# Two transformer models in one kernel: tiles moved by 32 bytes, query norms moved into the softmax exponent, steps cut in two

## What is computed

```python
def rmsnorm(x, g):
    y = xf * lax.rsqrt(jnp.mean(xf * xf, axis=-1, keepdims=True) + EPS)
    return y * g

def memory_cross(qm, k_mem, v_mem, q_gain, k_gain):     # layers 0 and 1, and alike in the second model
    q = rmsnorm(qm.reshape(b, s, N_MEM_HEADS, HEAD_DIM), q_gain) * HEAD_DIM ** -0.5
    k = rmsnorm(k_mem, k_gain)
    logits = jnp.einsum('bshd,bmhd->bhsm', q, k)
    p = jax.nn.softmax(logits, axis=-1)
    return jnp.einsum('bhsm,bmhd->bshd', p, v_mem)

# window attention of the second model: q and k normed, rotated, a sink in the softmax
    m = jnp.maximum(jnp.max(s, axis=-1, keepdims=True), sink)
    p = jnp.exp(s - m)
    denom = jnp.sum(p, axis=-1, keepdims=True) + jnp.exp(sink - m)
```

## Time and profile before

| | |
|---|---|
| median of 3 runs | 2280.51 us (2278.16 to 2287.36) |
| the profiled execution | 2279.7 us |
| its span | 2277.9 us |
| TensorE matmul busy | 2153.2 us (95%) |
| weight loads busy | 1778.0 us (78%) |
| VectorE busy | 1268.2 us (56%) |
| ScalarE busy | 934.3 us (41%) |
| POOL busy | 33.7 us (1%) |
| mean granted TensorE clock | 0.973 |
| DMA queue's share of the span | 25.4% |

### The profile page before, as it was taken

The page is one execution under the profiler, slowest core; times in us unless marked ns, Lnnn a source line. Parts: engine busy times, 40 slices in busy tenths (PEclk is TensorE's granted clock), DMA queues, the critical chain, the costliest instruction groups (busy, mean ns, idle before and its releaser), DMA issues.

```text
span 2277.9 us, 30665 instructions
## 1 busy us (share of the span) xinstructions
PE 2153.2 (95%) x11378; PEld 1778.0 (78%) x11378; DVE 1268.2 (56%) x2177; ACT 934.3 (41%) x1908; POOL 33.7 (1%) x71
## 2 busy tenths in 40 slices
PE   6899899999998777999999999999998779999999
PEld 6888688878888666888888888888887558888887
DVE  7545557736754664577377545344548735543542
ACT  6655444424435664444244333223343444332331
POOL 0000001000000000000000000000001000000000
PEclk9999899999999798999999999999999889999999
DMA  6211022332222000223322233323222003332332
GB/s 203 67 60 48 29 88 89 102 99 96 93 94 92 15 16 6 91 94 101 98 91 99 98 97 95 98 94 97 93 88 61 15 15 97 94 99 95 94 100 88
DMA packets 101669, 187.35 MB, mean 82 GB/s; under 512 B 11408, under 2 KB 12048, under 8 KB 101264
## 3 DMA queue, kind: packets, MB, share of 16 engines
q1 hardware_dynamic: 101520, 185.39, 25.4%
HBM read 183.25 MB, written 2.10 MB: 81 GB/s over the span
## 4 chain that ended last, share of the span: by engine, by line
PE 79%; DVE 8%; ACT 5%; issue 2%; DVEq 0%; ACTq 0%
PE PS L1391 22%; PE PS L1393 22%; PE PS L1392 22%; PE PS L1409 2%; PE PS L1410 2%; PE PS L1411 2%; PE PS L1511 2%; PE PS L1479 2%; PE PS L1497 2%; DVE WL L1553 1%; ACT PP L1865 1%; PE PS L1520 1%; DVE PSTAT L1650 1%; DVE RS L1542 1%; ACT WH L1796 1%
## 5 line engine op out<-in xcount | busy, mean ns | idle before, releaser
L1553 DVE TENSOR_TENSOR WL<-RAW,WH 128x512 fp32r<-128x512 f32 x681 | 458.6, 690 | 313.3 <-ACT WH L1796 291.7
L1391 PE MATMUL PS<-HNh,WH 128*128 128x512 f32 x1440 | 562.6, 391 | 0.7 <-DVE WL L1553 0.7
L1393 PE MATMUL PS<-HNh,WL 128*128 128x512 f32 x1440 | 560.3, 389 | 0.0
L1392 PE MATMUL PS<-HNl,WH 128*128 128x512 f32 x1440 | 560.2, 389 | 0.0
L1796 ACT ACTIVATE WH<-RAW 128x512 fp32r<-128x512 f32 x681 | 414.4, 626 | 331.7 <-PE PS L1393 223.0
L1391 PEld LDWEIGHTS PS<-HNh,WH 128*128 128x128 f32 x1440 | 270.3, 188 | 58.4 <-issue 2.4
L1392 PEld LDWEIGHTS PS<-HNl,WH 128*128 128x128 f32 x1440 | 270.3, 188 | 57.3 <-issue 1.2
L1393 PEld LDWEIGHTS PS<-HNh,WL 128*128 128x128 f32 x1440 | 270.3, 188 | 56.3
L1391 PE MATMUL PS<-Gh,WH 128*128 128x512 f32 x704 | 278.2, 395 | 0.8 <-DVE Gl L1707 0.8
L1393 PE MATMUL PS<-Gh,WL 128*128 128x512 f32 x704 | 278.1, 395 | 0.0
L1392 PE MATMUL PS<-Gl,WH 128*128 128x512 f32 x704 | 278.1, 395 | 0.0
(11 more groups left out here) (244 smaller groups left out, 2448.4 us busy)
## 6 DMA issues: line engine op xcount, KB each, us to landing
RAW<-in_w SPq DMA_DIRECT2D x681, 256.0 KB, 2.6
XT<-in_x SPq DMA_DIRECT2D x8, 256.0 KB, 5.3
MT<-in_mem SPq DMA_DIRECT2D x2, 1024.0 KB, 6.6
out_x<-XT SPq DMA_DIRECT2D x8, 256.0 KB, 2.0
PAR<-in_par SPq DMA_DIRECT2D x1, 207.0 KB, 7.9
CB<-in_cb SPq DMA_DIRECT2D x1, 100.0 KB, 7.8
PAR<-in_par SPq DMA_DIRECT2D x1, 84.5 KB, 2.0
CONST<-in_const SPq DMA_DIRECT2D x1, 65.0 KB, 6.0
```

What stands on the lines that cost most here:

```text
L1391: pe.matmul(out, wh, xh, start=(a["start"] and c == 0), stop=False)
L1392: pe.matmul(out, wh, xl, start=False, stop=False)
L1393: p = pe.matmul(out, wl, xh, start=False, stop=ends)
L1553: dve.tensor_tensor(l[:, :], r[:, :], h[:, :], ALU.subtract).then_inc(done.sem("split.dve"), 1)
```

## The change

1. **Places.** `FILL` gives 80 floats to a new tile `QR` [128, 5, 16] of roots; `FILL2` has 60 floats in place of 68. In the built program every tile from `KMH` to `PAR` then starts 32 bytes lower, at a multiple of 2048 (`KMH` 110592, `AOH` and `Gh` 137216, `AOL` 153600, `Gl` 159744). The tiles before `KMH` stay.
2. **Roots in the exponent.** Memory queries (all three) and window queries are turned as they come from `evac` (or from POOL's rotation), through a new function `unscaled`; their 10 `tnorm` are gone. The roots go to `QR`. `pmax` multiplies the negated maximum by the root, [128, 1] by [128, 1] (48 new instructions for memory pairs; for the 32 with sinks the `min` becomes one instruction that multiplies and takes the minimum), and `pexp` gets the root as a second pointer operand, the scale (80 exponents).
3. **Steps in two.** `rnorm` becomes `rlog` and `rnorm`, `qsplit` becomes `qhigh` and `qsplit`, `pmix` becomes `pmul` and `pmix`, with 0.9 to 1.5 units between, so VectorE has other steps in between.
4. **Smaller moves.** `recip` stands ahead of the copies of the fourth tile, not 0.1 units after. The latents' turns start 2.2, 4 and 5.5 units after the copy, not 0.2, 1.4 and 2.6.

```diff
-        sb("FILL", [128, 512 - 136 - 128 - 16 - 32])
+        QR = sb("QR", [128, 5, 16])
+        sb("FILL", [128, 512 - 136 - 128 - 16 - 32 - 80])
...
-        sb("FILL2", [128, 68])
+        sb("FILL2", [128, 60])
...
                 def rest():
+                    need(job.roots[1] if job.roots else [])
...
                 def copies():
+                    if i == 3:
+                        self.recip(n)
                     for x in range(2):
                         step(("pcopya", "pcopyb")[x], key + (x,), job=job, i=i, bank=banks[x], PT=PT[x], free=free)
-                    if i == 3:
-                        after(0.1, lambda: self.recip(n))
...
+                step("pmul", key, last=(self.id, n, 3), F=F, h=h, free=free)
+                after(1.2, lambda: step("pmix", key, F=F, h=h, l=l))
...
+        def roots(g, F, h, S, out=None, lag=1.5):
+            c = F.roots[h][0]
+            out = S[:, 3, c] if out is None else out[:, c]
+            step("rlog", (g, h), S=S, c=c, parts=F.roots[h][1],
+                 got=[("ssum.dve", (g, x)) for x in (range(len(F.squares)) if len(F.roots) == 1 else (h,))])
+            after(lag, lambda: step("rnorm", (g, h), S=S, c=c, out=out))
+
+        def unscaled(g, F, got, dsts, h, keep, lag=1.0):
+            if h == 0:
+                ss.take(g, [("rnorm.dve", (g, len(F.roots) - 1))])
+            squares(g, F, h, got(h))
+            ready_at = got(h)
+            if F.rots:
+                y, A, B, M = F.rots[h]
+                step("trope", (g, h), y=y, A=A, B=B, M=M, got=[("ssq.act", (g, h))])
+                ready_at = ("trope.pool", (g, h))
+            if h == len(F.squares) - 1:
+                for x in range(len(dsts)):
+                    after(lag + 1.5 * x, lambda x=x: turn(g, x, ready_at, dsts[x]))
+
+            def total():
+                sums(g, F, h, SS[ss.of[g]][:, 0, F.squares[h][3]], ss.before[g])
+                after(1.2, lambda: roots(g, F, h, SS[ss.of[g]], keep))
+            after(1.5, total)
...
-                step("qsplit", (g, x), src=PS[aux][0:rows, 0:n], h=h, l=l, gain=gain, free=tokens)
+                step("qhigh", (g, x), src=src, h=h, gain=gain, free=tokens)
+                after(0.9, lambda: step("qsplit", (g, x), src=src, h=h, l=l, gain=gain))
...
-                after(0.2 + 1.2 * x, lambda x=x, gain=gain: turn(g, x, ("evac.act", (g, 0)), (
+                after((2.2, 4, 5.5)[x], lambda x=x, gain=gain: turn(g, x, ("evac.act", (g, 0)), (
...
+                            m = stt(top, top, root(i, x), NSINK[:, h:h + 1], ALU.mult, ALU.min)
+                        else:
+                            m = dve.tensor_tensor(top, top, root(i, x), ALU.mult)
...
+                                   scale=a["job"].roots[0](i, x) if a["job"].roots else 1.0, accum_out=St[:, x, 1, i:i + 1]).then_inc(done.sem("pexp.act"), 1)
```

More of the change, by code:

```diff
@@ L739, in mix @@
                 need(free)
-                step("pmix", key, last=(self.id, n, 3), F=TMP[tmp.of["pmix", key]], h=AOH[:, job.chunk, :],
-                     l=AOL[:, job.chunk, :], free=free)
+                F, h, l = TMP[tmp.of["pmix", key]], AOH[:, job.chunk, :], AOL[:, job.chunk, :]
+                step("pmul", key, last=(self.id, n, 3), F=F, h=h, free=free)
+                after(1.2, lambda: step("pmix", key, F=F, h=h, l=l))
             def run(self):
@@ L955, in root @@
                 for h in list(range(len(F.roots)))[part]:
-                    step("rnorm", (g, h), S=S, c=F.roots[h][0], parts=F.roots[h][1],
-                         got=[("ssum.dve", (g, x)) for x in (range(len(F.squares)) if len(F.roots) == 1 else (h,))])
+                    roots(g, F, h, S)
                 after(lags[2], scale)
@@ L1031, in gates @@
             after(6, cum)
-        mq_got = [("qsplit.dve", (dense_at[0], c)) for c in range(2)]
+        g_mq0, mq_got = dense_at[0], [("qsplit.dve", (dense_at[0], c)) for c in range(2)]
         after(15.9, lambda: norm.columns(0))
@@ L1037, in mq_use @@
             gates(g)
-            heads(g, by_heads(Y, 4), lambda h: ("evac.act", (g, 0)), mq_chunks(0, par("mq0"))(Y))
+            for h in range(2):
+                unscaled(g, by_heads(Y, 4), lambda h: ("evac.act", (g, 0)), mq_chunks(0, par("mq0"))(Y), h, QR[:, 0, :])
         wide(norm, "fox", MQ_COLS, [PS[t][:, 0:268] for t in range(4)], range(4),
@@ L1202, in root @@
                 def root():
-                    step("rnorm", (g, 0), S=S, c=F.roots[0][0], parts=F.roots[0][1],
-                         got=[("ssum.dve", (g, x)) for x in range(len(F.squares))])
+                    roots(g, F, 0, S)
                     after(3, scale)
@@ L1317, in q_use @@
         def q_use(p):
-            return lambda g, Y, h: heads(
+            return lambda g, Y, h: unscaled(
                 g, by_heads(Y, 4, Q_ROT), lambda h: ("evac.act", (g, h)),
                 [(chunks_of(Y, 4, x), BQ[0][:, 2 * p + x, :], BQ[1][:, 2 * p + x, :], par("gq2"), lambda: [])
-                 for x in range(2)], h, h + 1)
+                 for x in range(2)], h, QR[:, 3 + p, :], 2.0)
         tiles = [(0, 128, [(0, MCAUS)])] + [(128 * (i - 1), 256, [(0, MPREV), (128, MCAUS)]) for i in range(1, 4)]
@@ L1325, in program @@
         jobs = [Pair([(BQ[0][r, n, :], BQ[1][r, n, :]) for r in (lo, hi)], [(BK[0][r, :], BK[1][r, :]) for r in (lo, hi)],
-                     VB[:, :, :], tiles, n, pair_got[n], sink=(n, 4 + n), wants=3) for n in range(4)] + mem_pairs(1, 4, mq_got)
+                     VB[:, :, :], tiles, n, pair_got[n], sink=(n, 4 + n), wants=3) for n in range(4)]
+        roots_of = {what: dense_at[0] + n for n, what in enumerate(BLK_GROUPS)}
+        for n, j in enumerate(jobs):
+            g = roots_of["q", 512 + 256 * (n // 2)]
+            j.scaled_by(QR[:, 3 + n // 2, :], lambda i, x, n=n: 4 * i + 2 * (n % 2) + x, [("rnorm.dve", (g, h)) for h in range(2)])
+        jobs += mem_pairs(1, 4, mq_got, QR[:, 2, :], roots_of["mq", 1280])
         for j in jobs[4:]:
@@ L1596, in vector @@
                     x.then_inc(done.sem("rnorm.in"), 1)
+                elif k == "rnorm":
+                    z, R = (a["S"][:, i, a["c"]] for i in (1, 2))
                     w.wait_ge(*done("rnorm.act", key))
```

65 lines of the change are left out of this document (38 added, 27 removed).

## The result

| | before | after |
|---|---|---|
| median of the runs, us | 2280.06 (4 runs) | 2246.02 (4 runs, 2243.52 to 2246.95) |
| ratio | | 0.9843, 95% interval 0.9820 to 0.9866 |
| profiled execution, us (its span) | 2279.7 (2277.9) | 2246.5 (2244.7) |
| last Gl matmul to first AOL matmul, latent layer | 693.0 to 902.8: 209.8 | 690.7 to 887.8: 197.1 |
| the same, second model | 1677.87 to 1858.12: 180.2 | 1655.24 to 1828.57: 173.3 |

The change gained 34 us, 1.5%; 2248 was forecast. Of the 33.2 us of the spans, 12.7 + 6.9 - 1.9 = 17.7 came from the attentions and 15.5 from everything else. The total is right.

The account below looks back on a forecast made before the run. TensorE's matmul-to-matmul time bounds the streaming stretches; waits between engines and a lowered clock bound the attentions. -18.4 - 2.4 - 7 - 5 = -32.8 from 2279.7 gives 2246.9, the median 0.8 higher: 2248 us, range 2234 to 2267.

Parts of the forecast that it names:

- Part 1: Tiles from KMH on start at multiples of 2048 bytes: Gl and AOL save 20.5 ns per weight tile, -18.4 us.
- part 4, cut steps: All attentions: cutting steps in two frees VectorE while ScalarE rounds; no gain counted where VectorE isn't the bound.
- part 4, reciprocal: All attentions: reciprocal ahead of the last turned tile's copies, TensorE's broadcast waits 0.45 us less each, -5 us.
- earlier memory tiles: Layer with latents: first memory score can come 8 us sooner, half of it counted, -4.2 us.
- hole: Second model's attention: memory tiles follow the last values at once, filling TensorE's 14.4 us before the memory scores, -8 us.
- VectorE's stretch: Second model's attention, where VectorE is the bound at first: six scalings go and waits in the root are filled, -4 us.
- rotation: Second model's attention: window queries' turns wait for POOL's rotation alone, +1 us where it is slow.
- products and pointers: Product of maximum and root plus the exponent's second pointer operand: +3.3 us in the latent layer, +4 in the second model.
- part 2, latents' turns: Layer with latents: turns spread wider among projection matmuls, TensorE's 1.49 us wait before the second goes, -1.5 us.
- a 512-column tile is exactly 2048 bytes: Argument that the 32-byte offset, not something else, makes Gl and AOL matmuls slower than HNl's.
- The first two rivals: The 32 bytes cost nothing (12%, 2266 us); the attentions give back nothing (13%, 2262 to 2267 us).
- Attention gives nothing back: Rival, 13%: longer memory and window tiles eat 12.7 us and gaps move to the exponent's wait; 2262 to 2267 us.

Follow-up runs that it names:

- hn_shifted: The changed kernel with 64 unused floats between XT and HNh, so HNh, HNl, RAW, WH and WL start 256 bytes past a multiple of 2048: 2243.1 us.
- places_only: The kernel before with FILL2 at 60 floats instead of 68, nothing else: 2262.9 us.
- norms_only: The kernel before with FILL2 at 60 floats and the moved norms; steps uncut, reciprocal and latents' turns as before: 2273.7 us.
- norms_as_before: The changed kernel with memory and local queries scaled ahead of their turns as before, no roots in maximum and exponent: 2238.1 us.
- steps_only: The kernel before with FILL2 at 60 floats, cut steps and the latents' spread turns; norms and reciprocal as before: 2248.3 us.
- norms_without_price: The changed kernel in its own order, without the maximum's product with the root and the exponent's second pointer operand (computes something else): 2238.2 us.

## Why the prediction was right, point by point

The forecast was 2248 and 2246.0 was measured. Part 1, more than half of it, was right by its mechanism; that the rest came to the right sum is luck. One path from before to after, each step by a measured pair: 2280.0, places 2262.9, cut steps and spread turns 2248.3, reciprocal 2238.1, norms 2246.0. Another order of the steps would share out the gains otherwise, as norms and cut steps overlap.

| term of the forecast | forecast us | measured us |
|---|---|---|
| part 1, places | -18.4 | -17 |
| part 4, cut steps | 0 | with the latents' turns -14.6; on top of norms and reciprocal -4.9 |
| part 4, reciprocal | -5 | -10 |
| parts 2, 3, norms: earlier memory tiles, hole, VectorE's stretch, rotation | -4.2 - 8 - 4 + 1 = -15.2 | 0 behind the cut steps |
| parts 2, 3, norms: products and pointers | +3.3 + 4 = +7.3 | +7.8 |
| part 2, latents' turns | -1.5 | +2.8 with uncut steps |

**Part 1** was right in mechanism and 1.4 us too large: AOL was taken at 20.5 ns per tile like Gl, 3.9 us; its three stages lose 3.4. Its argument that "a 512-column tile is exactly 2048 bytes" doesn't carry: in hn_shifted every HNl tile runs across a multiple of 2048 and still takes 389 ns.

**The price of the norms** was sized right in total (+7.3, measured +7.8), by luck in its parts. I had taken it as durations alone, added up: 3.3 in the latent layer and 4 in the second model. Measured are 6.0 in the latent layer, of which 1.6 lie where the added work is and 4.4 behind it at a lower clock; some 1.8 are left for all else.

**The gain of the norms** is one step that failed. I let the first memory score's 8 us count by half, and 8 of the 14.4 us of the hole. Both events came as forecast: the score 7.4 us sooner, the hole gone, centre without a wait. But both were set against the kernel before, and the cut steps of the same change take the same time away. In the latent layer the first causal pair starts 81 us behind the last Gl with or without the moved norms (86.2 in places_only, 84.3 in norms_only). In the second model, from the last window values to the first AOL matmul, places_only has 39.8 us, norms_only 33.6, norms_as_before 34.7 and the changed kernel 33.5: of the 6.2 us that the filled hole gives by itself 1.2 are left. The rest of that stretch in the changed kernel, from the first memory score on:

```profile
1795.60:1828.60 33.00, 22.64 (x152) 14.43 (x151) 17.19 (x50) 15.24 (x45) 0.00 (x0) 0.79 0.00 1
```

TensorE works 22.64 of 33 us at 0.79 there: the tiles went into the hole, and gaps stay between them, the longest in front of the last broadcast (3.19 us at 1819.83).

**"Free VectorE while ScalarE rounds: no gain counted where it isn't the bound"** is the other step that failed. VectorE isn't the bound by its busy share in the latent layer (119.70 of 212.5 us). But it takes its instructions in order, and for 32.7 us of its idle time it stood in the middle of a step with other work behind. I had read its busy time and not what its idle time held up.

**The reciprocal** was mis-sized by half: I counted 0.45 us per pair for what could move into the wait, and the whole wait went.

**POOL's rotations** of the window queries now take 1.74, 1.78, 1.32 and 1.31 us; I had one slow and the second row of rows 10, 0.86, as counter-evidence. By the rule of the Trainium skill (SBUF — State Buffer, Who interferes with whom) all four would be slow beside VectorE's taps, and here the trace agrees; in the trace before, the four took 1.73, 1.50, 0.86 and 0.87. What that cost was not separated.

The first two rivals were excluded: the 32 bytes cost 17 us, and the attentions gave back 17. But "Attention gives nothing back" was right about the norms, which eat 7.8 us and return next to nothing beside the cut steps; other parts paid for it. The sum came out at 2248 because 15.2 us too much gain on the norms stood against some 13 too little on the cut steps and spread turns and 5 too little on the reciprocal. The best version that ran and computes the right thing is norms_as_before, 2238.1 us: everything of the change except its moved norms, 8 us below the changed kernel.

## What to carry to other kernels

Where a step has a half on each of two in-order engines, issue them apart with the other engine's latency between them, even if neither engine is the bound: look up which engine's idle time ends with "waits for my other half", and what is queued behind. Starting work earlier pays only if the next thing to be late moves too; and a gap that one part of a change fills must not be counted again if another part closes it as well. When large moving tiles of equal shape show two durations, compare their start addresses first; it costs one line to test.

## What the hardware showed that I had not expected

**32 bytes.** A 512-column matmul whose moving tile starts 32 bytes past a multiple of 2048 takes 395 ns instead of 389 (Gl), and 256 bytes past it 389 (HNl). The Trainium skill (SBUF — State Buffer, Operand start alignment) asks for a multiple of the element's size and says that this is about legality, not speed; these runs show the speed.

**The same program, another clock.** The changed kernel and hn_shifted issue the same work in the same order. Their second model's stretches took 173.3 and 176.6 us, and their first AOL matmuls start at 280.6 and 285.1. The windows are set at the same distance from each one's last Gl matmul, and for the first attention from the start; the changed kernel first:

```profile
240.00:260.00 20.00, 17.64 (x126) 13.33 (x124) 10.61 (x25) 10.34 (x30) 0.00 (x0) 0.83 0.14 40
260.00:280.00 20.00, 14.85 (x129) 10.57 (x128) 9.55 (x23) 8.50 (x25) 0.00 (x0) 0.83 0.00 1
1755.60:1775.60 20.00, 16.55 (x166) 13.77 (x164) 17.00 (x46) 11.75 (x35) 0.00 (x0) 0.98 0.16 41
1775.60:1795.60 20.00, 15.27 (x128) 10.86 (x124) 13.14 (x36) 10.11 (x33) 0.00 (x0) 0.77 0.00 0
```

```profile
240.00:260.00 20.00, 17.64 (x123) 13.49 (x123) 10.59 (x26) 10.60 (x30) 0.00 (x0) 0.82 0.13 42
260.00:280.00 20.00, 15.45 (x111) 11.14 (x108) 8.41 (x20) 7.16 (x20) 0.00 (x0) 0.67 0.00 1
1759.70:1779.70 20.00, 16.56 (x166) 13.74 (x164) 17.04 (x46) 11.80 (x35) 0.00 (x0) 0.97 0.14 41
1779.70:1799.70 20.00, 15.59 (x101) 11.19 (x98) 11.83 (x33) 9.46 (x31) 0.00 (x0) 0.59 0.00 0
```

In the window ahead TensorE's busy time agrees to 0.01 us. Then the clock is granted at 0.77 on average in one execution and 0.59 in the other, and in the first attention at 0.83 and 0.67: the stretches differ by 3.3 us, the first attention by 4.5. The five runs of hn_shifted, all on one chip, lie between 2240.8 and 2253.9, and its profiled one is the slowest, so a difference between chips isn't needed for it. What decides when the clock falls, these traces don't show. So one profiled execution can't size a difference under some 5 us in a stretch with gaps. The medians can do better, and so can the latent stretch where several kernels of the same order agree on it. And in a stretch with gaps a change shows up in the matmuls as well as in the waits: 10.9 of 18.1 us in steps_only, 5.4 of 6.0 in norms_without_price, most of the latter behind the place that was changed.
